# A two-layer decoder trunk on one core: each 1 MB weight unit rounded, split and waited for in two halves

## What is computed

```python
for layer in range(DEPTH):                      # DEPTH = 2
    h = rms_norm(x, g_mix[layer])
    if layer % 2 == 0:
        x = x + attn_mixer(h, ...)              # dilated and sliding-window attention
        x = x + swiglu(rms_norm(x, g_ffn[layer]), w_gate_dense, w_up_dense, w_down_dense)
    else:
        x = x + hgrn2_mixer(h, ...)             # gated linear recurrence, chunks
        x = x + moe_swiglu(rms_norm(x, g_ffn[layer]), w_router, w_gate_moe, w_up_moe, w_down_moe)
return rms_norm(x, g_final)                     # moe: top 2 of 8 experts, d_ff = 3584
```

## Time and profile before

| | us |
|---|---|
| median of 3 runs | 1519.56 (1517.15 to 1523.24) |
| the profiled execution | 1519.06 |
| its span, first to last instruction | 1517.5 |
| PE busy | 1479.8 (98%) |
| DVE busy | 1191.2 (79%) |
| ACT busy | 984.8 (65%) |
| mean granted clock of TensorE | 0.99 of full |
| loop over the experts | 547 to 1499 |

### The profile page before, as it was taken

The page is one execution under the profiler, slowest core; times in us unless marked ns, Lnnn a source line. Parts: engine busy times, 40 slices in busy tenths (PEclk is TensorE's granted clock), DMA queues, the critical chain, the costliest instruction groups (busy, mean ns, idle before and its releaser), DMA issues.

```text
span 1517.5 us, 19512 instructions
## 1 busy us (share of the span) xinstructions
PE 1479.8 (98%) x7036; PEld 1223.3 (81%) x7036; DVE 1191.2 (79%) x1069; ACT 984.8 (65%) x866; POOL 112.3 (7%) x131
## 2 busy tenths in 40 slices
PE   6999999999999999999999999999999999999996
PEld 5767888888979888888888888888888888888884
DVE  7665544545685668988988988898898898898898
ACT  6556344445423567777777777777777787777775
POOL 0000300000232064000000000000000000002000
PEclk9999999999999989999999999999999999999998
DMA  9414896554543549999999999999999999999993
GB/s 343 158 56 133 290 413 234 191 175 133 170 135 111 166 163 389 406 386 387 384 364 389 396 359 386 394 358 383 397 361 381 394 371 371 391 377 372 388 407 130
DMA packets 200200, 462.54 MB, mean 305 GB/s; under 512 B 9000, under 2 KB 18272, under 8 KB 200160
## 3 DMA queue, kind: packets, MB, share of 16 engines
q1 hardware_dynamic: 191632, 436.26, 78.6%
q0 software_dynamic: 6912, 25.17, 4.2%
q10 hardware_dynamic: 1616, 0.56, 0.2%
HBM read 442.04 MB, written 19.92 MB: 304 GB/s over the span
## 4 chain that ended last, share of the span: by engine, by line
PE 89%; DVE 2%; ACT 2%; issue 1%; DVEq 0%; ACTq 0%
PE bank L1393 28%; PE bank L1395 27%; PE bank L1394 27%; PE bank L1560 2%; PE bank L1670 1%; ACT w_hi L544 1%; DVE w_lo L856 1%; PE bank L1797 0%; PE bank L1409 0%; PE bank L1763 0%; DVE X L1353 0%; PE bank L1527 0%; DVE work L1144 0%; PE bank L1751 0%; PE bank L1535 0%
## 5 line engine op out<-in xcount | busy, mean ns | idle before, releaser
L856 DVE TENSOR_TENSOR w_lo<-raw,w_hi 128x2048 fp32r<-128x2048 f32 x414 | 948.9, 2298 | 229.7 <-ACT w_hi L544 229.1
L544 ACT ACTIVATE w_hi<-raw 128x2048 fp32r<-128x2048 f32 x414 | 793.8, 1920 | 423.7 <-PE bank L1395 421.4
L1393 PE MATMUL bank<-w_hi,t_hi 128*128 128x512 f32 x1312 | 515.6, 393 | 5.1 <-DVE w_lo L856 3.4
L1395 PE MATMUL bank<-w_hi,t_lo 128*128 128x512 f32 x1312 | 510.1, 389 | 0.0
L1394 PE MATMUL bank<-w_lo,t_hi 128*128 128x512 f32 x1312 | 510.0, 389 | 0.0
L1393 PEld LDWEIGHTS bank<-w_hi,t_hi 128*128 128x128 f32 x1312 | 247.2, 188 | 59.6 <-issue 7.3
L1395 PEld LDWEIGHTS bank<-w_hi,t_lo 128*128 128x128 f32 x1312 | 247.0, 188 | 51.4
L1394 PEld LDWEIGHTS bank<-w_lo,t_hi 128*128 128x128 f32 x1312 | 247.2, 188 | 50.4 <-issue 1.0
L1393 PE MATMUL bank<-w_hi,h_hi 128*128 128x512 f32 x576 | 231.2, 401 | 0.0
L1395 PE MATMUL bank<-w_hi,h_lo 128*128 128x512 f32 x576 | 225.2, 391 | 0.0
L1394 PE MATMUL bank<-w_lo,h_hi 128*128 128x512 f32 x576 | 224.6, 390 | 0.0
(11 more groups left out here) (272 smaller groups left out, 818.0 us busy)
## 6 DMA issues: line engine op xcount, KB each, us to landing
raw<-in_w_gate_moe_dram SPq DMA_DIRECT2D x114, 1024.0 KB, 8.0
raw<-in_w_up_moe_dram SPq DMA_DIRECT2D x113, 1024.0 KB, 8.1
raw<-in_w_down_moe_dram SPq DMA_DIRECT2D x112, 1024.0 KB, 7.4
raw<-in_w_in_rec_dram SPq DMA_DIRECT2D x16, 1024.0 KB, 5.5
raw<-in_w_gate_dense_dram SPq DMA_DIRECT2D x14, 1024.0 KB, 5.8
raw<-in_w_up_dense_dram SPq DMA_DIRECT2D x14, 1024.0 KB, 5.2
raw<-in_w_down_dense_dram SPq DMA_DIRECT2D x14, 1024.0 KB, 4.8
raw<-in_w_in_attn_dram SPq DMA_DIRECT2D x9, 1024.0 KB, 13.7
```

What stands on the lines that cost most here:

```text
L544: act.activation(w_hi[:, (u - 1) % SPL, :], raw[:, r, :], ACT.Copy).then_inc(hi_done, 1)
L856: dve.tensor_tensor(w_lo[:, s, :], raw[:, r, :], w_hi[:, s, :].bitcast(F32), ALU.subtract).then_inc(lo_done, 1)
L1393: pe.matmul(o, lh, rh, start=start, stop=False)
L1395: return pe.matmul(o, ll, rh, start=False, stop=stop)
```

## The change

Nothing is added to what is computed. ACT's copy becomes two instructions of 128x1024 to a unit; the first counts on a new semaphore `hi_half`, the second on `hi_done`. DVE's subtraction becomes two of 128x1024: the first waits on `hi_half` and counts on `lo_half`, the second waits on `hi_done` and counts on `lo_done`. TensorE waits on `lo_half` at the start of a unit and on `lo_done` in its middle (`unit_rest`), at each of the places where units are used. SP still waits on `lo_done`, and ACT still on `unit_done`.

```diff
@@ scalar: split_to
-                    act.activation(w_hi[:, (u - 1) % SPL, :], raw[:, r, :], ACT.Copy).then_inc(hi_done, 1)
+                    for half, signal in ((slice(0, UNIT // 2), hi_half), (slice(UNIT // 2, UNIT), hi_done)):
+                        act.activation(w_hi[:, (u - 1) % SPL, half], raw[:, r, half], ACT.Copy).then_inc(signal, 1)
@@ vector: split_to
-                    dve.wait_ge(hi_done, n.step("unit"))
+                    n.step("unit")
                     s, r = (u - 1) % SPL, (u - 1) % RAW
-                    dve.tensor_tensor(w_lo[:, s, :], raw[:, r, :], w_hi[:, s, :].bitcast(F32),
-                                      ALU.subtract).then_inc(lo_done, 1)
+                    for half, ready, signal in ((slice(0, UNIT // 2), hi_half, lo_half),
+                                                (slice(UNIT // 2, UNIT), hi_done, lo_done)):
+                        dve.wait_ge(ready, n.at("unit"))
+                        dve.tensor_tensor(w_lo[:, s, half], raw[:, r, half], w_hi[:, s, half].bitcast(F32),
+                                          ALU.subtract).then_inc(signal, 1)
@@ tensor: unit
-                pe.wait_ge(lo_done, n.step("unit"))
+                pe.wait_ge(lo_half, n.step("unit"))
                 return s
+
+            def unit_rest():
+
+                pe.wait_ge(lo_done, n.at("unit"))
@@ tensor: col_half
                 for k in range(per):
+                    if k == per // 2:
+                        unit_rest()
@@ tensor: down_units
                     for c in range(2):
+                        if c:
+                            unit_rest()
@@ tensor: narrow units
                         for k in range(KC):
+                            if k == KC // 2 and c == 0:
+                                unit_rest()
```

More of the change, by code:

```diff
@@ L223, in build @@
         hi_done, lo_done = sem("hi_done"), sem("lo_done")
+        hi_half, lo_half = sem("hi_half"), sem("lo_half")
         unit_done = sem("unit_done")
@@ L1483, in filler @@
                     for k in range(KC):
+                        if k == KC // 2:
+                            unit_rest()
                         ws = slice(k * 256, (k + 1) * 256)
@@ L1610, in _ @@
                 for c in range(2):
+                    if m < c:
+                        unit_rest()
                     for t in range(TT):
@@ L1630, in _ @@
                             drained(TB[part])
+                            if part == 2:
+                                unit_rest()
                             if part == 0:
```

## The result

| | before | changed |
|---|---|---|
| median of 8 runs each, us | 1519.8 (1517.15 to 1523.24) | 1512.39 (1508.84 to 1514.24) |
| ratio | | 0.9947 [0.9937, 0.9958] |
| the profiled execution | 1519.06 | 1508.84 |
| its span | 1517.5 | 1507.2 |

The change wins 7.4 us between the medians, 8.1 by the ratio. The forecast was 9.0. One caution for all that follows: the changed kernel's profiled execution is the fastest of its eight, and part of the 10.3 us by which its span is shorter is luck.

The account below looks back on a forecast made before the run. PE's own work was taken to bound the loop; only its standing still for the split could be won. 1519.06 - 2.0 - 5.0 - 1.2 - 0.8 = 1510.1, stated as a median of 1510.6 us, range 1508.0 to 1518.0.

Parts of the forecast that it names:

- (b): Narrow units, about 388 to 438 us: shorter direct wait, faster DVE chain, no clock fall; 5.0 us won, between 1.5 and 5.5.
- (c): Expert loop: seven round starts no longer delayed by late `w_lo`, 0.17 us each; 1.2 us won, between 0 and 2.
- ACT never waits for a load: Expert loop: SP's load waits for `lo_done`, up to 0.8 us earlier, would have no consequence.
- The length of the halves: Every split: DVE's half 1.22 us, its pair 2.35 against 2.29 whole; ACT's two halves +0.1 us a unit.
- The wait in the middle: PE's wait inside each unit, 414 times: 0 us, upper end 21; rival that it costs PE, 1531.6 us, chance 0.07.
- the border between units: Expert loop: PE's wait for `w_lo` between units shows no gap, 0.227 us as inside, so a mid-unit wait should cost nothing.
- (a): Start, up to rope: first matmul 1.9 us earlier, capped by rope's 1.0 us of slack; 2.0 us won, between 1.0 and 2.2.
- I take 5.35: Narrow units' DVE chain: 5.35 us a pass instead of 5.79, so 3.1 us earlier at 426.66.
- The clock at 429: Narrow units: PE standing still only 0.7 us, so no fall to half clock; 1.6 us won.
- (d): End: the last chain, through the split of an unused unit, gets shorter; 0.8 us won, between 0.5 and 0.9.
- all behind it is DVE's own: End: after the last split only DVE's own work follows, so its 0.8 us would carry through.

Follow-up runs that it names:

- second profile: The changed kernel run and profiled again with no edit: 1511.28 us, ratio 0.9935 to the kernel before.
- e5: Changed kernel with POOL's products among the narrow units cut to eight elements, so output not the reference's: 1508.3 us, ratio 0.9918.
- e8: Changed kernel with DVE's copy ahead of a round's last split, and three of POOL's four products waiting for DVE's split: 1509.38 us, ratio 0.9930.
- e4: Changed kernel with whole units inside the expert loop and halves only ahead of it: 1515.41 us, ratio 0.9965.
- e9_before_copy_first: The kernel before, whole units, with only DVE's copy moved ahead of the round's last split: 1519.41 us, ratio 0.9996.
- e1: Changed kernel with PE waiting for the whole unit at its start and nowhere in its middle: 1513.89 us, ratio 0.9953.

## Why the prediction was right, and where it was wrong

The time, 1510.6 for 1512.39, and the sign were right, and so is the mechanism: the gain comes where PE stood still for the split. That the total came so near is in part luck. In the second profile (b) is 2.1 us short and (c) 1.5 us over, and 1.6 us of what did come is a stretch of the clock that can't be claimed for the change. Two slips of the working changed nothing: 35.3 units and not 36.4 fall into 100 us of the loop (42 in 118.85), and "ACT never waits for a load" does not hold in every execution (in the second profile it waited 9.2 us, 15 times; the rounds are as long). Term by term:

**The length of the halves: right.** 1227 ns for DVE (1.22), a pair of 2.36 (2.35), ACT 1054 ns (1.06). The Trainium skill, "VectorE: DVE Perf Modes", the TRN2 errata section, has (N + 151) / 0.96 ns, which makes an estimate of 1224 ns for 1024 elements, and the trace agrees with that duration. The 0.157 us for each further instruction, which the prediction worked out from it, is not what the engine loses here: DVE's busy time rose by 1219.7 - 1191.2 = 28.5 us for 414 more instructions, 0.069 each, and by 54.0 more for 828 more in quarters, 0.065 each (both with the stretches beside POOL in them), for one starts up to 0.09 us before the last ends.

**The wait in the middle: right.** Zero was forecast, with 21 us as the upper end. The changed kernel and the one without these waits have the same rounds, so the border between units, which carried the argument, was the right row to read.

**(a) The start: right.** The first matmul runs at 14.63, in a profile in which ACT's split begins 0.23 later than before (12.17 against 11.94): 14.4, as forecast. 1.5 and 1.7 us are left behind rope, for 2.0, in the first with the matmuls at the slow pace and in the second at the fast one.

**(b) The narrow units: half wrong, and this is the forecast's largest miss.** The direct wait went as worked out, 1.7 for 1.55 us. The step that failed is the one from "1.4 (1156 to 1157, or 1167 to 1170), then 2.35, so 5.15, or 5.5 where POOL slows DVE" to "I take 5.35". The chain came each 5.59 us, since the pair took 3.0 to 3.2 us beside POOL. DVE's own steps were even shorter than I had them (4.99 us in run e5, not 5.15), but POOL's share was 0.65 to 0.85 us and not 0.2 to 0.35. By pass: 0.20 us won for the 0.44 forecast, 1.4 us in six passes, and that is the whole miss of this stretch, since all of it ends in PE's wait at `own_products`, 2.20 us for 0.7.

Why POOL costs more than before can be read from single instructions. Before, POOL's product of 128x256 started 0.31 us ahead of DVE's split, because DVE still waited for ACT: POOL took its normal 0.85 us, and the split, held up at its start, took 2.70 for 2.29. With ACT's half DVE goes first, 0.16 us ahead of POOL. DVE's two halves of the pair at 420.84, one row each (count, busy, mean ns, idle before):

```profile
L861 DVE TENSOR_TENSOR w_lo<-raw,w_hi 128x1024 fp32r<-128x1024 f32 x1 | 1.2, 1217 | 0.0
...
L861 DVE TENSOR_TENSOR w_lo<-raw,w_hi 128x1024 fp32r<-128x1024 f32 x1 | 1.9, 1867 | 0.0
```

The first half is undisturbed. POOL's product, begun at 421.00, ends at 422.76, 0.7 us after the first half's end at 422.06; its normal time is 0.85. The second half, begun at 421.98, takes 0.64 us longer. That is as if they took turns, an instruction each. In run e5, POOL's product of eight elements beside an undisturbed half took 1.12 us (424.45 to 425.57, the half runs from 424.29 to 425.51), which is waiting and hardly work. With POOL put behind the split (e8) the term gave 2.0 us, with its work taken out (e5) 2.4. The Trainium skill, "SBUF — State Buffer", the section on SBUF's two separate sides, has this mechanism: DVE, when it reads two inputs from SBUF, and GpSimd, when it reads SBUF, need a shared pair of ports, and the one that starts first has it for its whole instruction while the other waits. The traces agree: POOL's product beside an undisturbed half took 1.76 instead of 0.85 us. They also show what cutting an instruction does there: the end of a piece lets POOL in.

The same collision is behind the loss at 438: the pair at 431.81 takes 2.77 us beside POOL's line 425, and PE then waits 0.96 us for line 1200, where it had waited 0.5. In run e5 POOL is done before that split begins, and 0.8 us are won there.

**(b) The clock at 429: right in size, wrong in its reason.** I wrote that PE would stand still for 0.7 us and the clock would therefore stay up. PE stood still for 2.20 us and it stayed up all the same, in the changed kernel and in its second profile:

```profile
426.00:429.40 3.40, 3.40 (x14) 2.44 (x15) 3.40 (x3) 1.00 (x2) 2.68 (x2) 1.00 0.72 280
```

In run e4, after the same code up to there and a wait of 2.22 us, it fell:

```profile
426.60:430.00 3.40, 3.40 (x8) 2.35 (x7) 3.40 (x4) 0.61 (x1) 3.08 (x2) 0.50 0.56 217
```

The kernel before shows it both ways too. Run `e9_before_copy_first` has its code up to the last units of a round. Both wait at `own_products` alike, 2.05 and 2.07 us; before the clock fell behind the wait, in e9 it did not (first row before, second e9):

```profile
429.30:432.70 3.40, 3.40 (x8) 2.32 (x7) 3.02 (x3) 0.50 (x1) 3.09 (x2) 0.50 0.56 218
```

```profile
430.20:433.60 3.40, 3.34 (x13) 2.45 (x14) 2.98 (x3) 1.08 (x1) 2.51 (x2) 1.00 0.72 281
```

Between 429 and 434 e9 wins the same 1.6 us on the profile before, without the change. The places at half clock move from execution to execution, each worth 1 to 3 us, and are part of the spread of the runs. So nothing shows that these 1.6 us belong to the change; without them, and without the 2.8 us of luck in the first, both profiles hold some 6 us. How often the clock falls there with and without the change stays open. A gain of the clock should have stood in the range and not in the sum.

**(c) The loop: right in kind, too small.** 0.38 us a round and 2.7 in all for 1.2. I had priced one border in a round at 0.17 us. It gives 0.25, and the waits of the earlier trace rows come twice in a round: the first down unit gives 0.05 to 0.11 more. Run e4 ties both to the halves.

**(d) The end: right in size, its path only half right.** 0.7 for 0.8. DVE's copy did come 0.8 us earlier against the end of the loop. But "all behind it is DVE's own" was wrong: ACT's chain to `ST` does not get shorter by the halves, ends 0.2 us after the copy, and now starts the matmuls at the end. Moving the copy wins nothing.

**What stays open.** 0.3 us are lost between 46 and 134 in both profiles, and I don't know why. The same stretch differs by more in executions with unchanged code: in e9 it is 1.3 us longer than before, with a stretch at half clock, 0.50, from 85.1 to 88.5 us.

## What to carry to other kernels

Cutting a producer's step in two pays where a consumer waits for the first piece of a chain of two engines, and next to nothing where the work is ahead anyway; the piece that mattered most here was the first engine's, not the last one's. Cost it at every place with what will run beside it afterwards: an earlier start can turn the order in which two engines get at the same port, and here that took back 2 us, which came back when POOL was made to wait. Where the clock or the spread of runs can give or take as much as a term, keep it out of the sum, and profile the same kernel twice before reading a gain of a few us.

## What the runs showed of the hardware

- Waits that are met before they are reached cost nothing that can be measured inside a run of matmuls: 42 a round, under 0.02 us together (changed kernel against e1).
- DVE's subtraction and POOL's products, all in SBUF, held each other up by whole instructions: the pair took 2.75 to 3.35 us instead of 2.35, and a product of POOL 1.76 instead of 0.85.
- One more DVE instruction to a unit cost DVE 0.06 to 0.07 us: 2.29 whole, 2.36 in halves, 2.50 in quarters, 2.73 in eighths.
- The more pieces, the dearer POOL's company: the same unit beside line 407 took 2.86 us whole, 3.20 in halves and 3.96 in quarters.
- The granted clock's stretches at half speed fall differently in executions of the same code: 6.8 or 13.6 us near 530, and one of 3.4 us or none behind a wait of 2.05 to 2.07 us at 429.
